# Expert outputs added to a table in DRAM by indirect DMA, and three up steps of the next block taken into a block

## The reference

```
h2 = rms_norm_2(x, norm2_g) * (1 + scale2) + shift2
scores = sigmoid(t @ w_router); 8 of 64 experts per token, gates g
per block of up to 128 tokens of one expert e:
    out = swiglu(t[toks], w1[e], w3[e], w2[e]) * gs      # up 1024 -> 256 twice, down 256 -> 1024
routed = segment_sum(out, row_tok)                       # each token sums its 8 experts
x = x + gate2 * (routed + swiglu(t, ws1, ws3, ws2))      # the shared expert
```

## Time and profile before

| what | us |
|---|---|
| median of 3 runs (range) | 1110.96 (1106.64 to 1120.57) |
| the profiled execution | 1107.02 |
| its span, first to last instruction | 1105.2 |
| one block in the loop (900.52 to 912.09) | 11.57 |
| mean granted clock of TensorE | 0.956 |

### The profile page before, as it was taken

How to read it: one execution, slowest core, us unless ns; L and a number is a source line. 1 busy time by engine, 2 the same in 40 slices (tenths; PEclk the granted TensorE clock), 3 DMA queues, 4 the chain that set the end, 5 groups by cost and what they waited for, 6 DMA issues and landing times. The chain is left out here.

```text
span 1105.2 us, 15988 instructions
## 1 busy us (share of the span) xinstructions
PE 1012.0 (92%) x4922; PEld 809.8 (73%) x4922; DVE 801.0 (72%) x1334; ACT 583.5 (53%) x887; POOL 203.6 (18%) x235
## 2 busy tenths in 40 slices
PE   5999999997999898878879688899999999999994
PEld 4778878786776675567668577677888888888883
DVE  4677887666754443466596654799999999999995
ACT  4555554434434332335335321677777777777772
POOL 4142220001000000021130000423223233232230
PEclk9999999998999898988899798999999999999997
DMA  9776776648535242534334212988888888888882
GB/s 320 262 265 220 256 239 226 220 161 274 197 96 173 90 153 77 192 97 153 125 104 153 77 38 102 355 306 344 317 317 345 307 341 334 312 343 318 329 337 79
DMA packets 91203, 247.35 MB, mean 224 GB/s; under 512 B 13244, under 2 KB 23925, under 8 KB 77842
## 3 DMA queue, kind: packets, MB, share of 16 engines
q1 hardware_dynamic: 84578, 226.36, 57.3%
q0 software_dynamic: 6000, 19.96, 4.7%
q10 hardware_dynamic: 576, 0.41, 0.1%
HBM read 244.27 MB, written 2.29 MB: 223 GB/s over the span
## 5 line engine op out<-in xcount | busy, mean ns | idle before, releaser
L1716 PE MATMUL bank<-w_hi,a_hi 128*128 128x512 f32 (+2 forms) x512 | 211.0, 412 | 17.8 <-issue 6.4
L1716 PE MATMUL bank<-w_lo,a_hi 128*128 128x512 f32 (+2 forms) x512 | 202.7, 396 | 0.0
L1716 PE MATMUL bank<-w_hi,a_lo 128*128 128x512 f32 (+2 forms) x512 | 202.5, 395 | 0.0
L1195 DVE TENSOR_TENSOR w_lo<-ring,w_hi 128x1024 fp32r<-128x1024 f32 (+2 forms) x136 | 156.9, 1180 | 62.0 <-ACT w_hi L916 57.5
L916 ACT ACTIVATE w_hi<-ring 128x1024 fp32r<-128x1024 f32 (+2 forms) x140 | 141.3, 1024 | 97.1 <-PE bank L1716 92.2
L1585 DVE TENSOR_TENSOR up_lo<-raw_weights,up_hi 128x1024 fp32r<-128x1024 f32 x136 | 164.4, 1250 | 3.0
L1716 PEld LDWEIGHTS bank<-w_hi,a_hi 128*128 128x128 f32 x512 | 101.0, 197 | 48.7 <-issue 21.9
L1076 ACT ACTIVATE up_hi<-raw_weights 128x1024 fp32r<-128x1024 f32 x136 | 135.8, 1050 | 0.0
L1716 PEld LDWEIGHTS bank<-w_hi,a_lo 128*128 128x128 f32 x512 | 100.8, 197 | 20.7
L771 POOL TENSOR_SCALAR mean_squares<-mean_squares 128x8 f32<-128x8 f32 (+2 forms) x32 | 10.0, 313 | 571.6 <-ACT logits L878 306.3
L1716 PEld LDWEIGHTS bank<-w_lo,a_hi 128*128 128x128 f32 x512 | 101.3, 198 | 19.0 <-issue 1.0
(11 more groups left out here) (257 smaller groups left out, 1824.9 us busy)
## 6 DMA issues: line engine op xcount, KB each, us to landing
raw_weights<-in_w_dram SPq DMA_DIRECT2D x102, 1024.0 KB, 6.9
ring<-in_w_in_dram SPq DMA_DIRECT2D x58, 1024.0 KB, 5.3
merged<-in_w_ada_dram SPq DMA_DIRECT2D x96, 256.0 KB, 5.3
ring<-in_w_out_dram SPq DMA_DIRECT2D x8, 1024.0 KB, 5.2
ring<-in_w_branch_dram SPq DMA_DIRECT2D x6, 1024.0 KB, 4.8
bias<-rel_rows SPq DMA_DIRECT2D x40, 128.0 KB, 5.1
block_rows<-place_rows SPq DMA_DIRECT2D x34, 128.0 KB, 8.6
ring<-in_ws_dram SPq DMA_DIRECT2D x2, 1024.0 KB, 6.0
```

Of the source, the lines that this page charges most:

```text
L1195: dve.tensor_tensor(w_parts[1][:, 2 * p:2 * p + 2, 0:w], view(JOB[it[1:3]], kind)[:, 2 * p:2 * p + 2, :], w_parts[0][:, 2 * p:2 * p + 2, 0 ...
L1716: mm = pe.matmul(ps[:, 0:w], a_parts[za][:, k, t * P:(t + 1) * P], w_parts[zw][:, k, 0:w], start=start, stop=stop)
```

## The change

A table `routed_rows` of 384 rows by 1024 in DRAM is cleared in the router stage with three DMAs of POOL. After each block, POOL issues an indirect DMA that adds the block's 128 gated output rows to the table (`add_rows`); unused rows go to 128 dump rows behind the tokens'. The `put` matrices, their loads, `y_lo` and all scatter matmuls are gone. ACT writes one tile `y_add` and waits for the preceding add to have landed before it writes again. At the end SP loads the table back, and DVE multiplies and adds it to x. The shared expert's part of x is now added by DVE ahead of the blocks, which frees the banks, so that the up product alternates between two banks. PE does steps 0 to 2 of block i+1 inside block i, and only steps 3 to 7 of block i at its head. The second half of `down_lo` moves from DVE to POOL. The gather skips unused rows. `find_tokens` stands between up steps 5 and 6.

```diff
--- before.py
+++ after.py
+C_COL, C_EXP, C_THR, C_NONE, C_N = 776, 777, 778, 779, 780
 FAR = 1000.0
+NO_TOKEN = 1024.0
...
+ADDED_FROM = 16 * (NT + 1)
...
-        place_rows = nc.dram_tensor("place_rows", (NV, TOK), F32, kind="Internal").ap()
+        routed_rows = nc.dram_tensor("routed_rows", (TOK + P, DM), F32, kind="Internal").ap()
...
-        y_hi = sb("y_hi", [P, DM], F32R, operands)
-        y_lo = sb("y_lo", [P, DM], F32R, operands)
+        y_add = sb("y_add", [P, DM], F32, operands)
+        routed = sb("routed", [P, NT, DM], F32, operands)
...
-        hidden_b, turned_b = bank[4], bank[5]
-
-        gather_b = [y_b[0], y_b[1], hidden_b, turned_b]
+        turned_b = bank[5]
+        found_b = turned_b[:, TOK:TOK + 4]
+
+        def hidden(r):
+
+            return (bank[4], bank[1])[r % 2]
...
-            sp.wait_ge(S("rows_turned"), 1)
-            sp.dma_start(place_rows, prow[:, :]).then_inc(S("places_stored"), 16)
...
-                        sp.wait_ge(S("down_lo"), 2 * i - 2)
+                        for f in range(FT):
+                            sp.wait_ge(S(f"down_lo_{f}"), i - 1)
                         load_down(r, load_up(i, r))
-                        load_places(i, r)
+                        load_columns(i + 3, (r + 3) % BODY)
+            sp.wait_ge(S("rows_added"), 16 * n_work + ADDED_FROM)
+            sp.dma_start(routed[:, :, :], routed_rows[0:TOK, :].rearrange("(t p) n -> p t n", p=P)).then_inc(S("routed_loaded"), 16)
...
+                    bank_taken(gp, USE["out2", 1, 1])
+                    for r in range(2):
+                        gp.memset(xg[:, r, :], 0.0).then_inc(S("rows_cleared"), 1)
+                    gp.wait_ge(S("rows_cleared"), 2)
+                    for z in range(NT + 1):
+                        gp.dma_start(routed_rows[z * P:(z + 1) * P, :], xg[:, z % 2, :]).then_inc(S("rows_added"), 16)
...
+                if isinstance(i, int):
+                    gp.wait_ge(S("rows_added"), ADDED_FROM)
...
+                                      bounds_check=TOK - 1, oob_is_err=False)\
                   .then_inc(S(f"rows_gathered_{r}"), 16)
+
+            def add_rows(i, r):
+
+                gp.wait_ge(S("y_gated"), 2 * i + 2)
+                gp.sem_inc(S("pool_begun"), 1)
+                gp.indirect_dma_start(out=routed_rows, out_offset=bass.IndirectOffsetOnAxis(ap=tok[:, r, 0:1], axis=0),
+                                      in_=y_add[:, :], in_offset=None, compute_op=ALU.add)\
+                  .then_inc(S("rows_added"), 16)
...
+            make_pick(2, 2, 1)
...
-                        make_pick(i + 2, after, m4 + 1 + (r + 2) // BODY)
-
-                        gp.wait_ge(S("consts_loaded"), 16)
-                        gp.wait_ge(S("block_done"), i + 1)
-                        gp.wait_ge(S(f"row_loaded_{r}"), 16 * (m4 + 1))
+                        gp.wait_ge(S("down_hi"), 2 * i + 2)
                         gp.sem_inc(S("pool_begun"), 1)
-                        gp.tensor_scalar(put[:, :], row4[:, r, :], consts[:, C_COL:C_COL + 1], None, ALU.is_equal)\
-                          .then_inc(S("put_ready"), 1)
+                        gp.tensor_tensor(down_lo[:, 1, :], raw[:, 1 - r % 2][:, UP + DM:UP + 2 * DM],
+                                         down_hi[:, 1, :].bitcast(F32), ALU.subtract).then_inc(S("down_lo_1"), 1)
                         gather_rows(i + 2, after)
+
+                        make_pick(i + 3, (r + 3) % BODY, m4 + 1 + (r + 3) // BODY)
+                        add_rows(i, r)
...
-                        act.wait_ge(S("block_done"), i + 1)
+                        act.wait_ge(S("rows_added"), 16 * i + ADDED_FROM)
                         for hf in range(2):
-
                             act.wait_ge(S(f"down_{hf}"), i + 1)
-                            act.activation(y_hi[:, hf * CH:(hf + 1) * CH], y_b[hf][:, :], ACT.Copy, scale=gcol[:, r, 0:1])\
-                               .then_inc(S(f"y_hi_{hf}"), 1)
+                            act.activation(y_add[:, hf * CH:hf * CH + CH], y_b[hf][:, :], ACT.Copy, scale=gcol[:, r, 0:1])\
+                               .then_inc(S("y_gated"), 1)
...
-                    dve.wait_ge(S("ranks_turned"), 1)
-                    dve.tensor_copy(prow[:, :], y_b[0][:, 0:TOK]).then_inc(S("rows_turned"), 1)
...
+                dve.tensor_scalar(tok[:, r, :], found[:, 2:3], NO_TOKEN, consts[:, C_NONE:C_NONE + 1], ALU.add, ALU.min)\
+                   .then_inc(S("tokens_ready"), 1)
...
+            dve.wait_ge(S("block_done"), 1)
+            for hf in (1, 0):
+                for t in range(NT):
+                    n = NT * (1 - hf) + t
+                    o = x[:, t, hf * CH:hf * CH + CH]
+                    if n >= NT:
+                        dve.wait_ge(S("shared_added"), n - 1)
+                    dve.tensor_tensor(qn[:, t, :], acc_b[2 * t + hf][:, :], gate_bc[:, 1, hf * CH:hf * CH + CH], ALU.mult)\
+                       .then_inc(S("shared_gated"), 1)
+                    dve.wait_ge(S("shared_gated"), n + 1)
+                    dve.tensor_tensor(o, o, qn[:, t, :], ALU.add).then_inc(S("shared_added"), 1)
...
-                        for f in range(FT):
-                            dve.wait_ge(S("down_hi"), 2 * i + f + 1)
-                            dve.tensor_tensor(down_lo[:, f, :], raw[:, 1 - r % 2][:, UP + f * DM:UP + (f + 1) * DM],
-                                              down_hi[:, f, :].bitcast(F32), ALU.subtract).then_inc(S("down_lo"), 1)
+                        dve.wait_ge(S("down_hi"), 2 * i + 1)
+                        dve.tensor_tensor(down_lo[:, 0, :], raw[:, 1 - r % 2][:, UP:UP + DM],
+                                          down_hi[:, 0, :].bitcast(F32), ALU.subtract).then_inc(S("down_lo_0"), 1)
                         for m in range(2):
                             rest_of_up_weights(i + 1, nxt, 0, m)
+                        take_tokens(i + 2, (r + 2) % BODY, found_b)
                         dve.wait_ge(S("silu_done"), i + 1)
-                        dve.tensor_tensor(he, hs[:, 0, :], hidden_b[:, ED:2 * ED], ALU.mult).then_inc(S("h_done"), 1)
+                        dve.tensor_tensor(he, hs[:, 0, :], hidden(r)[:, ED:2 * ED], ALU.mult).then_inc(S("h_done"), 1)
                         rest_of_rows(i + 1)
                         dve.wait_ge(S("h_hi_ready"), i + 1)
                         dve.tensor_tensor(h_lo[:, :, :], turned_b[:, 0:ED].rearrange("p (f n) -> p f n", f=FT),
                                           h_hi[:, :, :].bitcast(F32), ALU.subtract).then_inc(S("h_lo_ready"), 1)
-                        take_tokens(i + 2, (r + 2) % BODY)
                         for m in range(2):
                             rest_of_up_weights(i + 1, nxt, 1, m)
-                        for hf in range(2):
-
-                            dve.wait_ge(S(f"y_hi_{hf}"), i + 1)
-                            c = slice(hf * CH, (hf + 1) * CH)
-                            dve.scalar_tensor_tensor(out=y_lo[:, c], in0=y_b[hf][:, :], scalar=gcol[:, r, 0:1],
-                                                     in1=y_hi[:, c].bitcast(F32), op0=ALU.mult, op1=ALU.subtract)\
-                               .then_inc(S(f"y_lo_{hf}"), 1)
-
-            dve.wait_ge(S("experts_summed"), 1)
+            dve.wait_ge(S("shared_added"), 2 * NT)
+            dve.wait_ge(S("routed_loaded"), 16)
             for t in range(NT):
                 for hf in range(2):
+                    n = 2 * t + hf
                     tmp = qn[:, hf, :]
                     o = x[:, t, hf * CH:hf * CH + CH]
-                    dve.tensor_tensor(tmp, acc_b[2 * t + hf][:, :], gate_bc[:, 1, hf * CH:hf * CH + CH], ALU.mult)\
-                       .then_inc(S("final_step"), 1)
-                    dve.wait_ge(S("final_step"), 2 * t + hf + 1)
...
+                    dve.tensor_tensor(tmp, routed[:, t, hf * CH:hf * CH + CH], gate_bc[:, 1, hf * CH:hf * CH + CH],
+                                      ALU.mult).then_inc(S("final_step"), 1)
+                    dve.wait_ge(S("final_step"), n + 1)
...
-            for t in range(NT):
-                mm = pe.transpose(y_b[0][:, t * P:(t + 1) * P], ranks[:, t, :], ident)
-            mm.then_inc(S("ranks_turned"), 1)
...
-            def scatter(hf, n):
-
-                pe.wait_ge(S(f"y_lo_{hf}"), n)
-                for t in range(NT):
-                    for part in (y_hi, y_lo):
-                        mm = pe.matmul(acc_b[2 * t + hf][:, :], put[:, t * P:(t + 1) * P],
-                                       part[:, hf * CH:hf * CH + CH], start=False, stop=False, skip_group_check=True)
-                return mm
-
             DOWN_PASSES = [(f, 0, z) for f in range(FT) for z in range(2)] + [(f, 1, 0) for f in range(FT)]
 
-            def expert_block(i, r, nxt_loads):
-
-                nxt = (r + 1) % BODY
-                pe.wait_ge(S("tokens_ready"), i + 2)
-                for k in range(KT):
+            def up_steps(i, r, ks):
+
+                for k in ks:
```

(36 more changed lines are left out.)

44 lines of the change are left out of this document (20 added, 24 removed).

## The result

| | before | after |
|---|---|---|
| time, median (lowest to highest) | 1109.1 us (1106.64 to 1120.57) | 1300.11 us (1292.47 to 1304.84) |
| profiled execution: time, span, granted clock | 1107.02, 1105.2, 0.956 | 1304.84, 1303.0, 0.865 |

The ratio of the means is 1.1692, 95% interval 1.1585 to 1.1799: 17% slower. Forecast were 1256 us, with 1300 as the upper end of the range, so the measured time stands just at that end.

A forecast was written before the change was run, and what follows sets the result against it. PE bounded the kernel, but would now wait for x_block_lo in every block: 713.45 + 6 - 0.4, plus 32 × 16.04 = 513.3, plus 22, plus 1.8 outside the span = 1256 us; range 1165 to 1300.

The forecast's parts named there:

- another rival: Low clock for nearly all PE work after the gap and part of the up steps: 1290 to 1330 us; chance 0.10.
- the clock term: TensorE's clock falls after standing still 4.6 us in every block: 1.7 us more per block, period 16.04 us.
- PE finds x_block_lo late: Behind the turned rows PE, there at D+4.50 (D: down product's end), waits for x_block_lo until D+9.13; period 14.34 us.
- The rival in which the clock holds: POOL excludes DVE, but the clock holds through 4.6 us gaps: period 14.34, total 1202 us; chance 0.15.
- POOL's subtraction excludes DVE: POOL's down_lo subtraction delays DVE's up_lo by a whole instruction: 1.73 us per block, period 14.34 instead of 12.6.
- the down_lo taken from DVE: Moving it off DVE in each block gives next to nothing, because DVE waits for ACT there anyway.
- The add is hidden: Issued by POOL about D+1.15 in 1.4 us, landing taken as 7.0 us, needed about D+14.5: reserve 6 us.
- The head: Up to the first block's end: DVE's added multiplies and adds and a little contention, +6 us on 713.45.
- The tail: From the last down product to the span's end: add, read-back, DVE and output, 22 us against 18.9, so +3.
- The bare sum: Taking 1.86 us of PE work out of each of 32 periods gains 60 us if PE's operands are ready.

The follow-up runs named there:

- e7: e3 with the accumulating transfer of each block left out, so the output lacks the experts' part: 1094.59 us.
- e3: Changed kernel with all up steps back at the block's head and both halves of down_lo on DVE: 1124.6 us, ratio 1.0102 to the kernel before.
- e10: e1 with nine unused matmuls per block added in TensorE's wait for x_block_lo: 1172.74 us.
- e4: Changed kernel with 18 unused matmuls per block added where TensorE waits for x_block_lo: 1211.45 us.
- e1: Changed kernel with the second half of down_lo back on DVE, inner up steps kept: 1190.94 us.
- e2: Changed kernel with all eight up steps at the block's head, GpSimd's subtraction kept: 1186.48 us.
- e5: Changed kernel with the accumulating transfer of each block left out, so the output lacks the experts' part: 1255.28 us.
- e8: e3 with the shared experts' additions moved from before the loop to behind the last block: 1117.05 us.
- e11: e8 with only rows holding a token added, and up weights loaded as soon as up_lo is done: 1119.93 us.

## Why the prediction was right in kind and 44 us short

The periods form a ladder, each rung one run: PE's own work 9.7 and its waits for h 10.96 (e7); the add's traffic 11.47 (e3); step 0 behind x_block_lo 13.03 (e10); GpSimd's subtraction 14.49 (e4); the clock 17.06.

The measured 1300 falls into the band of another rival (1290 to 1330), but for another reason: that rival took the clock term for larger than 2.7 us, and it was 2.57. Most of the rest was lost ahead of the first block's end.

- **PE finds x_block_lo late**: right. The prediction had the wait end at D+9.13, measured 9.24, and a period of 14.34 without the clock, measured 14.49 (e4). The rival in which the clock holds (1202) is e4 with 1211.
- **POOL's subtraction excludes DVE**: right, 4.22 against 2.36 us for the same pair: 1.86 us of delay, where 1.73 was taken. The prediction held that the down_lo taken from DVE gives next to nothing. It gave 0.4: up_lo begins at D+3.76, and at D+4.15 in e1. So the period shows 1.46 (e4 to e10). The Trainium skill's rule ("SBUF — State Buffer", Who interferes with whom) agrees with this: the one that comes second is blocked for the whole instruction of the other. Here the first up_lo takes 3.08 us, until 1.1 us after POOL's end.
- **The clock term**, 1.7 us, was too small: 2.57 (e4), which is the upper of the two cases that the earlier trace rows showed, a low stretch of 6.83 us, where I had taken a value between them. 32 × (17.06 - 16.04) = 33 us of the miss are the period's: 28 from this term, 5 from the 14.34. It isn't a constant, and it doesn't follow the length of one wait alone: 0.71 us a block in e1 (one wait of 2.9 us, every second block keeps its clock), 1.2 in e2 (waits of 1.7 and 0.5 us, six of 31 blocks keep it), 2.57 with the wait of 4.5.
- **The add is hidden**: true for its landing (6.2 us against 7.0 guessed; nobody waits), false for its issue. I had POOL issue it at D+1.15 in 1.4 us, through before the subtraction; it began at D+1.71 and took 1.62. Price 17.06 - 15.94 = 1.12 us per block (e5), 36 us in all. It doesn't show as a separate miss: the issue moved the wait's end by 0.39, but the predicted D+9.13 was 0.28 too late for a block without it (8.85 in e5), so two errors met there by luck, and the rest is part of the clock term.
- **The head**, +6 on 713.45, was 22.4: the first block ended at 735.9. 8.4 us of it had been lost before the first changed instruction. DVE's first gated product (qn) ahead of the router, which no version touches nor anything before it, began at 638.6 to 642.0 us in six traces besides the 639.4 of before, and at 647.0 to 648.0 in the other six, the changed kernel's 647.8 among them. The clock accounts for it: before that product the later group had stood 92.2 us at the lower level, the earlier one 75.1 to 78.5. From there to the work list ten of the twelve took 43.7 to 44.0 us with the clearing in them (before 44.2), and two 47.2 to 47.3, the changed kernel being one: 3.0 more. So the clearing costs nothing, as predicted; these 11.4 us are the spread of one execution to the next. From the work list on, the changed first block took 11.0 us more than before, where 5.6 was forecast. 4.6 are the additions (e3 to e8), and one of them took 2.64 us beside POOL's subtraction instead of 0.69; the rest wasn't taken apart.
- **The tail**: 22 forecast, 21.2 measured (1281.8 to 1303.0).
- **The bare sum**, a gain of 60 us or a period of 9.7, needs other work in the places that the scatter leaves. With steps 0 to 2 there PE waits for x_block_lo, without them it waits 1.2 us a block for h (e7): no version here came under 10.9. The prediction didn't name the second wait.

Sum of the misses: 33 + 17 - 1 = 49, against 1304.84 - 1256 = 49 for the profiled execution; the median lies 5 us lower. Not settled: whether the inner steps can pay if x_block_lo is made before up_lo; that wasn't tried.

## What to carry to other kernels

Before work is moved ahead inside a loop, follow the operand that it now needs first (here x_block_lo) back to the loop's start; filling a wait of TensorE is only a gain if the wait it opens elsewhere is shorter. A wait of TensorE can cost its length and the work behind it at half clock: measure the second part by filling the wait with matmuls whose result isn't used. Before work is taken out of an engine, look at what it was hiding: the scatter stood where PE would else have waited for h. Of a software-issued transfer count three things: its landing, its issue time on GpSimd ahead of what stands next there, and which big transfers were issued just before it.

The adds can't be left to overlap each other: the Trainium skill ("DMA: Bandwidth & Descriptors", Rules for kernel authors) says that a write landing between an accumulation's read and write of the same bytes is lost, so each add has to wait for the one before. No run here shows it.

## What the runs showed that I had not expected

- An accumulating indirect transfer of 128 rows of 4 KB landed in 6.2 us, faster than a gather: 7.0 for as many rows before the change, and 8.8 in the changed kernel, where the gather skips unused rows. The add wasn't issued just behind the weights there; 1.05 us behind 2 MB of weights it took 10.5. The gather went the other way: 8.5 us in e3 and e7, with and without the add, and 5.7 in e11, where it was no longer issued just behind the weights.
- The queues' shares can add up to more than the engines' time (101.6% in e3), and 28 of 31 blocks still took less than 12.3 us, eight of them no more than 10.98. At 77% (e7) all took 10.94 to 11.02.
- A wait of 2.9 us in every block (e1) dropped the clock in every second one only, and with most of it filled (e10) it stood at 1.00 through the whole stretch read; waits of 1.7 and 0.5 us (e2) dropped it in 25 blocks of 31.
